# Keys of the first two token pairs from tokens times scale, the shift's part added as a row

## The reference

```
xm = rmsnorm(x, norm_w) * (1 + scale) + shift          # 4096 x 1024
k  = rope2d(xm @ w_k)                                  # 512 of w_in's columns, heads of 64
v  = xm @ w_v
state_b = sum over the tokens of the other half of gamma^m * k_m (x) v_m
```

## Time and profile before

| | |
|---|---|
| time, median of 3 runs | 877.23 us (876.34 to 927.11) |
| the profiled execution: time, span of its slowest core | 877.3 us, 875.7 us |
| spans of the eight cores | 870.9 to 875.7 us |
| PE busy | 800.4 us, 91% of the span |
| DVE, ACT, POOL busy | 465.4, 360.7, 330.8 us |
| chain that ended last | PE 80%, DMA 6%, ACT 5%, DVE 4%, issue 3% |
| of it, loads of ada_w | 4% |

### The profile page before, as it was taken

How to read it: one execution, slowest core, us unless ns; L and a number is a source line. 1 busy time by engine, 2 the same in 40 slices (tenths; PEclk the granted TensorE clock), 3 DMA queues, 4 the chain that set the end, 5 groups by cost and what they waited for, 6 DMA issues and landing times.

```text
span 875.7 us, 14323 instructions; the slowest of 8 cores (870.9 to 875.7 us)
## 1 busy us (share of the span) xinstructions
PE 800.4 (91%) x4504; PEld 384.6 (44%) x4504; DVE 465.4 (53%) x1090; ACT 360.7 (41%) x642; POOL 330.8 (38%) x372
## 2 busy tenths in 40 slices
PE   0079999999988999999999999999999999999996
PEld 0045445444444444444444444444444444444443
DVE  2457534899778777767623442344256412333435
ACT  3589646898466435343432122122212211222222
POOL 0136523676578454545410302221143143232333
PEclk9999999999999999999999999999999999999999
DMA  8999955774391221315551715325015260034233
GB/s 244 280 290 187 212 111 97 175 156 104 55 162 35 38 54 29 55 29 78 81 86 42 118 34 96 52 46 97 1 23 122 81 112 1 25 118 148 72 120 145
DMA packets 72256, 87.83 MB, mean 100 GB/s; under 512 B 51691, under 2 KB 57963, under 8 KB 70518
## 3 DMA queue, kind: packets, MB, share of 16 engines
q1 hardware_dynamic: 66854, 59.65, 25.9%
q0 software_dynamic: 5328, 27.27, 18.9%
HBM read 93.72 MB, written 8.39 MB: 117 GB/s over the span
## 4 chain that ended last, share of the span: by engine, by line
PE 80%; DMA 6%; ACT 5%; DVE 4%; issue 3%; POOL 1%; SPq 1%; DVEq 0%; ACTq 0%; POOLq 0%
PE P L1006 53%; PE P L588 13%; PE P L1303 6%; DMA wt<-ada_w 4%; ACT tm L983 2%; DMA cm<-rope 2%; PE P L707 2%; DVE vb L1021 1%; ACT st L905 1%; PE P L828 1%; PE P L648 1%; PE P L946 1%; PE P L475 1%; PE P L691 1%; PE P L947 1%
## 5 line engine op out<-in xcount | busy, mean ns | idle before, releaser
L1006 PE MATMUL P<-xmt,vb 128*128 128x512 bf16 x1280 | 283.1, 379 | 2.8 <-DVE wt L1202 1.8
L1006 PEld LDWEIGHTS P<-xmt,vb 128*128 128x128 bf16 x1280 | 124.5, 98 | 152.6 <-issue 3.7
L588 PE MATMUL P<-wt,xmt 128*128 128x512 bf16 x688 | 158.3, 382 | 4.4 <-ACT xmt L509 3.4
L1006 PE MATMUL P<-xmt,wt 128*128 128x512 bf16 x512 | 118.8, 380 | 1.1 <-ACT wt L1157 0.9
L1205 POOL TENSOR_TENSOR kz<-tm,wt 128x1024 bf16<-128x1024 f32 x16 | 45.7, 2857 | 162.4 <-DVE wt L1202 162.4
L588 PEld LDWEIGHTS P<-wt,xmt 128*128 128x128 bf16 x688 | 65.2, 98 | 79.8 <-issue 7.5
L1006 PEld LDWEIGHTS P<-xmt,wt 128*128 128x128 bf16 x512 | 49.3, 98 | 58.3 <-issue 2.7
L1282 DVE SCALAR_TENSOR_TENSOR tm<-tm,P 128x512 f32<-128x512 f32 x32 | 22.0, 687 | 87.6 <-PE P L1006 87.6
L1158 DVE TENSOR_TENSOR wt<-P,wt 128x512 f32<-128x512 f32 x32 | 22.1, 692 | 83.4 <-ACT wt L1157 62.8
L1284 POOL TENSOR_TENSOR st<-st,tm 128x512 bf16<-128x512 bf16 x32 | 39.8, 1243 | 65.8 <-DVE tm L1282 65.8
L1006 PE MATMUL P<-vb,wt 128*128 128x512 bf16 x256 | 61.4, 386 | 0.0
(11 more groups left out here) (176 smaller groups left out, 1110.8 us busy)
## 6 DMA issues: line engine op xcount, KB each, us to landing
kz<-x SPq DMA_DIRECT2D x24, 512.0 KB, 9.2
wt<-x SPq DMA_DIRECT2D x24, 512.0 KB, 4.6
vb<-w_conv POOLq DMA_DIRECT2D x16, 512.0 KB, 8.3
out<-wt SPq DMA_DIRECT2D x15, 512.0 KB, 2.7
st<-ada_w SPq DMA_DIRECT2D x2, 2048.0 KB, 14.1
wt<-ada_w SPq DMA_DIRECT2D x2, 2048.0 KB, 28.8
vb<-w_mix POOLq DMA_DIRECT2D x8, 512.0 KB, 11.1
cm<-rope SPq DMA_DIRECT2D x33, 64.0 KB, 3.9
```

Source lines behind the costliest of these rows:

```text
L588: ins = e.matmul(pf(bank)[:, 0:wid], lhsT=lhs_x(ch, k), rhs=w[:, k, c0_:c0_ + wid], start=(k == 0), stop=(k == 7))
L1006: ins = e.matmul(pf(bank), lhsT=lhs(k), rhs=rhs(k), start=(k == 0), stop=(k == 7))
```

## The change

Blocks 2 and 3 of `ada_w` (the scale) are loaded first, blocks 0 and 1 (the shift) last, and the buffers are assigned anew so that block 2 lies where the `xc` buffers 4 to 7 come. The key weights are loaded as float32 by SP in two halves (`wk_load`) and cast by DVE and ACT (`wk_cast`), in place of the casting DMA of POOL. `dpn` is loaded later; `mask_tables` is cut in two, `mask_exponents` and the rest.

For pairs 0 and 1 `f_aff_noshift` multiplies by the scale only. `k_open` projects a chunk in two groups of four matmuls and leaves the accumulation open in banks 2 to 5. When the shift is known, it is split into two bfloat16 columns (`shi`), `f_kb` multiplies them with the key weights in 8 matmuls to two rows of 512 in bank 6, the rows are split again into `kbh` and `kbl`, and `k_close` adds them to each open bank by two matmuls with a matrix of ones. Then the four chunks are rotated by `o_krope`. The loop over p begins at 2; `g_acc` of pair 0 and of pair 1 both stand in its first round. `xmTh`, the convolution's neighbour columns, is computed by its own small operations. Pairs 2 to 7 are computed as before.

```diff
--- before.py
+++ after.py
@@ -283,7 +283,14 @@
         xc = [buf(f"xc{i}", (SZ if i < 4 else WZB - 16384) + i * 4096, [128, 1024], F32) for i in range(8)]
         xso = [buf(f"xso{i}", VB + i * 2048, [128, 1024], BF16) for i in range(16)]
         kfo = [buf(f"kfo{i}", KT + i * 1024, [128, 512], BF16) for i in range(16)]
-        adaf = [buf(f"adaf{i}", o, [128, 4096], F32) for i, o in enumerate((ST, ST + 16384, WB, WZB))]
+        adaf = [buf(f"adaf{i}", o, [128, 4096], F32) for i, o in enumerate((ST + 16384, WB, WZB, ST))]
+        wkf = [buf(f"wkf{i}", XMT + 16384 + i * 8192, [128, 2048], F32) for i in range(2)]
+
+        shi = at(TMP + 14336, [128, 8, 2], BF16)
+        own("shi", TMP + 14336, 32)
+        kbh = buf("kbh", TMP + 12288, [128, 512], BF16)
+        kbl = buf("kbl", TMP + 13312, [128, 512], BF16)
+        xh2 = buf("xh2", TMP + 14400, [128, 8, 2], F32)
         adas = [buf(f"ada{i}", KT + (i % 2) * 8192, [128, 8, 512], BF16) for i in range(4)] + \
                [buf(f"ada{4 + i}", WB + i * 8192, [128, 8, 512], BF16) for i in range(2)]
         gT = at(ST, [128, 8, 576], BF16)
@@ -356,10 +363,15 @@
             P.op("dve", lambda e: e.tensor_copy(out=v[:, 0:2048], in_=adaf[i][:, 0:2048]), reads=[f"adaf{i}"], writes=[nm[0]])
             P.op("act", lambda e: e.activation(out=v[:, 2048:4096], in_=adaf[i][:, 2048:4096], func=AF.Copy), reads=[f"adaf{i}"], writes=[nm[1]])
 
-        P.dma("sp", lambda e: e.dma_start(out=dpn, in_=dpn_d[:, :]), "dpn", writes=["dpn"])
-        for i in range(3):
-            ada_load(i)
-        P.dma("pool", lambda e: e.dma_start(out=wk, in_=wk_d.rearrange("p (k c) -> p k c", k=8)), "wk", reads=["adaf2"], writes=["wk"])
+        def wk_load(q):
+            P.dma("sp", lambda e: e.dma_start(out=wkf[q], in_=wk_d[:, q * 2048:(q + 1) * 2048]), f"wkf{q}", writes=[f"wkf{q}"])
+
+        def wk_cast(q):
+            v = wk[:, 4 * q:4 * q + 4, :].rearrange("p k c -> p (k c)")
+            own(f"wk{q}d", WGB + q * 4096, 2048)
+            own(f"wk{q}a", WGB + q * 4096 + 2048, 2048)
+            P.op("dve", lambda e: e.tensor_copy(out=v[:, 0:1024], in_=wkf[q][:, 0:1024]), reads=[f"wkf{q}"], writes=[f"wk{q}d"])
+            P.op("act", lambda e: e.activation(out=v[:, 1024:2048], in_=wkf[q][:, 1024:2048], func=AF.Copy), reads=[f"wkf{q}"], writes=[f"wk{q}a"])
 
         P.op("dve", lambda e: e.tensor_copy(out=identb, in_=identf), reads=["identf"], writes=["identb"])
 
@@ -401,7 +413,7 @@
 
         P.op("act", lambda e: e.activation(out=scT, in_=vT[:, :, 0:2], func=AF.Silu), reads=["vT"], writes=["scT"])
 
-        def mask_tables():
+        def mask_exponents():
             def f_marg0(e):
                 ins = None
                 for h in range(8):
@@ -427,8 +439,10 @@
                     ins = e.scalar_tensor_tensor(out=marg[:, h, :], in0=iv, scalar=col, in1=marg[:, h, :], op0=ALU.mult, op1=ALU.subtract)
                 return ins
             P.op("dve", f_marg3, reads=["nlg", "dpn", "marg"], writes=["marg"])
+            P.op("dve", lambda e: e.tensor_scalar(out=diag, in0=identf, scalar1=1.0, scalar2=None, op0=ALU.add), reads=["identf"], writes=["diag"])
+
+        def mask_tables():
             P.op("act", lambda e: e.activation(out=marg, in_=marg, func=AF.Exp), reads=["marg"], writes=["marg"])
-            P.op("dve", lambda e: e.tensor_scalar(out=diag, in0=identf, scalar1=1.0, scalar2=None, op0=ALU.add), reads=["identf"], writes=["diag"])
 
             def f_mt(e):
                 ins = None
@@ -482,6 +496,27 @@
                 blk, j = ch["xm"]
                 P.dma("sp", lambda e, ch=ch, blk=blk, j=j: e.dma_start_transpose(out=xm[blk][:, :, j * 128:(j + 1) * 128], in_=ch["xs"][0]),
                       f"tx{ch['n'] % 4}", reads=[ch["xs"][1]] + list(after), writes=[f"xm{blk}_{j}"])
+
+        def f_aff_noshift(pair):
+            blk, j0 = pair[0]["xm"]
+            dst = xm[blk]
+            names = [f"xm{blk}_{j0}", f"xm{blk}_{j0 + 1}"]
+
+            def f_d(e):
+                ins = None
+                for k in range(4):
+                    ins = e.tensor_scalar(out=dst[:, k, j0 * 128:(j0 + 2) * 128], in0=pb(0)[:, k * 256:(k + 1) * 256],
+                                          scalar1=Amod[:, k, 0:1], scalar2=None, op0=ALU.mult)
+                return ins
+
+            def f_a(e):
+                ins = None
+                for k in range(4, 8):
+                    ins = e.activation(out=dst[:, k, j0 * 128:(j0 + 2) * 128], in_=pb(1)[:, (k - 4) * 256:(k - 3) * 256],
+                                       func=AF.Copy, scale=Amod[:, k, 0:1])
+                return ins
+            P.op("dve", f_d, reads=["Amod", "P0"], writes=[n_ + "d" for n_ in names])
+            P.op("act", f_a, reads=["Amod", "P1"], writes=[n_ + "a" for n_ in names])
 
         def f_aff(pair, inplace=False):
             r = 1 if pair[0]["kind"] == "ctx" else 0
@@ -611,33 +646,94 @@
                 return ins
             P.op("dve", f_modT, reads=[f"P{bank}", "vT"], writes=[name])
 
+
+        ada_load(2)
         load2(0)
+        ada_load(3)
+        wk_load(0)
+        wk_load(1)
+        P.dma("sp", lambda e: e.dma_start(out=dpn, in_=dpn_d[:, :]), "dpn", writes=["dpn"])
+        load2(1)
+        ada_load(0)
         rope2(0)
-        ada_load(3)
-        load2(1)
         rope2(1)
+        ada_load(1)
+        ada_cast(2)
+        ada_mm(2, 7, 0)
+        load2(2)
+        rope2(2)
+        load2(3)
+        sq2(0)
+        scale2(0)
+        load2(4)
+        f_tp(other[0])
+        for half in range(2):
+            P.op("dve", lambda e, half=half: e.tensor_copy(out=xh2[:, half * 4:half * 4 + 4, :],
+                                                           in_=pb(half).rearrange("p (a b) -> p a b", a=4)[:, :, 0:2]),
+                 reads=[f"P{half}"], writes=["xh2"])
+        ada_cast(3)
+        ada_mm(3, 7, 0)
+        modT_part((1,), "modT1", 7, 0)
+        P.op("dve", lambda e: e.tensor_scalar(out=Amod, in0=modT[:, 8:16, :], scalar1=1.0, scalar2=None, op0=ALU.add),
+             reads=["modT1"], writes=["Amod"])
+        P.op("dve", lambda e: e.tensor_tensor(out=Amod, in0=Amod, in1=vT[:, :, 2:3].broadcast_to([128, 8, 2]), op=ALU.mult),
+             reads=["Amod", "vT"], writes=["Amod"])
+        wk_cast(0)
+        f_aff_noshift(other[0])
+        wk_cast(1)
+
+        def k_open(ch, bank, part):
+            def f(e):
+                ins = None
+                for k in range(4 * part, 4 * part + 4):
+                    ins = e.matmul(pf(bank), lhsT=lhs_x(ch, k), rhs=wk[:, k, :], start=(k == 0), stop=False)
+                return ins
+            P.op("pe", f, reads=[xname(ch) + "da"[part], f"wk{part}d", f"wk{part}a"], writes=[f"P{bank}"])
+
+        def k_close(bank):
+            def f(e):
+                e.matmul(pf(bank), lhsT=onesb[0:2, :], rhs=kbh[0:2, :], start=False, stop=False)
+                return e.matmul(pf(bank), lhsT=onesb[0:2, :], rhs=kbl[0:2, :], start=False, stop=True)
+            P.op("pe", f, reads=["onesb", "kbh", "kbl"], writes=[f"P{bank}"])
+
+        for part in range(2):
+            for c in range(2):
+                k_open(other[0][c], 2 + c, part)
+        mask_exponents()
+        sq2(1)
+        scale2(1)
+        load2(5)
+        f_tp(other[1])
         ada_cast(0)
         ada_mm(0, 7, 0)
+        f_aff_noshift(other[1])
+        for part in range(2):
+            for c in range(2):
+                k_open(other[1][c], 4 + c, part)
+        mask_tables()
         ada_cast(1)
         ada_mm(1, 7, 0)
-        mask_tables()
-        ada_cast(2)
-        ada_mm(2, 7, 0)
-        sq2(0)
-        scale2(0)
-        ada_cast(3)
-        ada_mm(3, 7, 0)
-        load2(2)
-        load2(3)
-        modT_part((0, 1), "modT", 7, 0)
-        P.op("dve", lambda e: e.tensor_scalar(out=Amod, in0=modT[:, 8:16, :], scalar1=1.0, scalar2=None, op0=ALU.add),
-             reads=["modT"], writes=["Amod"])
-        P.op("dve", lambda e: e.tensor_tensor(out=Amod, in0=Amod, in1=vT[:, :, 2:3].broadcast_to([128, 8, 2]), op=ALU.mult),
-             reads=["Amod", "vT"], writes=["Amod"])
-        f_tp(other[0])
-        f_aff(other[0])
-        sq2(1)
-        scale2(1)
+        modT_part((0,), "modT", 7, 0)
+
+        def f_shi(e):
+            return e.tensor_copy(out=shi[:, :, 0], in_=modT[:, 0:8, 0])
+
+        def f_slo(e):
+            return e.tensor_tensor(out=shi[:, :, 1], in0=modT[:, 0:8, 0], in1=shi[:, :, 0], op=ALU.subtract)
+        P.op("dve", f_shi, reads=["modT"], writes=["shi"])
+        P.op("dve", f_slo, reads=["modT", "shi"], writes=["shi"])
+
+        def f_kb(e):
+            ins = None
+            for k in range(8):
+                ins = e.matmul(pf(6)[0:2, :], lhsT=shi[:, k, :], rhs=wk[:, k, :], start=(k == 0), stop=(k == 7))
+            return ins
+        P.op("pe", f_kb, reads=["shi", "wk"], writes=["P6"])
+        P.op("dve", lambda e: e.tensor_copy(out=kbh[0:2, :], in_=pf(6)[0:2, :]), reads=["P6"], writes=["kbh"])
```

(29 more changed lines are left out.)

## The result

| | before | after |
|---|---|---|
| time, median of the runs on one chip | 877.16 us | 892.57 us |
| ratio, 95% interval | | 1.0177 [1.0162, 1.0191] |
| profiled execution: time, span of its slowest core | 877.3, 875.7 us | 892.8, 891.3 us |
| PE busy | 800.4 us | 813.7 us |

What follows compares the result with a forecast made beforehand. PE was taken to bound the kernel from about 60 us on, so the head's delay counts whole: pair 3's first K projection moves from 70.05 to 79.7, and 877.3 + 9.7 = 887.0 us, range 880 to 893.

Steps and rivals of the forecast that it cites:

- POOL's pair behind two `kfo`: Pair 2's two small POOL operations queue behind kfo0 and kfo1, delaying its scale; K of pair 2 starts at 68.75.
- the marker: Start of the first K projection of pair 3: 70.05 us before, forecast 79.7, so +9.7 us.
- rival 3: Slower by more than 2%: starved PE stays below 2.4 GHz in the pass, +36 us, 923; chance 0.04.
- T = 47.6: Landing of the last ada_w block, now block 1, in us; the middle between 46.6 and 48.6.
- counting rope rows by bytes, 0.26 MB at the queue's rate: In the load queue ahead of the last ada_w block, the rope rows were counted as 0.26 MB at 0.32 MB/us.
- The step that the casting load cost no more than a plain one: In the load queue: 0.32 MB/us with the cast load beside, 0.314 and 0.34 without, so no gain from SP.
- PE has just run K of pair 1, so warm: The shift row's 8 matmuls behind T run at full pace, 1.89 us; the other end adds 1.7.
- as the second POOL wait covers it: Ahead of the marker, half pace costs little: pair 3 at 79.7, warm 79.2, since POOL's second wait hides it.
- Behind the marker all is as before, per pair: From pair 3 to the end a pair costs 6.07 us and the shift of 9.7 reaches the end whole.
- for the `kfo` alone: DVE and GpSimd blocking could delay each kfo beside a rope up to 0.4, sum 1.5 higher; nothing was added.
- The pass's ragged end: Idle time at 103.47 and a low clock from 105 to 110 could win back 3.5 us at most.
- The two 2-partition operations: Behind the shift's row, two DVE operations on 2 partitions of 512 from PSUM: 0.6 + 0.7 us with gaps.

Runs made afterwards that it cites:

- the third experiment: The changed kernel with the four rope rows of pairs 0 and 1 loaded behind the last ada_w block: 889.70 us, ratio 1.0153.
- e1: The changed kernel with sq2(2) and scale2(2) written ahead of the ropes of chunks 0 and 1: 888.96 us, ratio 1.0152.
- e2: The changed kernel without the shift's row, its split and the closings (keys of pairs 0 and 1 lack the shift): 888.02 us, ratio 1.0136.
- e7: The changed kernel with useless matmuls (12, 3, 6 and 28) put into PE's idle time: 893.19 us, ratio 1.0190.
- the fourth experiment: The kernel before with only w_k loaded as float32 on SP behind the fourth ada_w block, cast by DVE and ACT: 875.92 us, ratio 1.0003.
- the ninth experiment: The changed kernel with one added dependency, POOL's multiply in chunk 5's retention waiting for DVE's eighth operation: ratio 1.0157.
- the fourth to sixth: On the fourth experiment, the fifth makes POOL's multiply wait for DVE's eighth operation: 874.25 us, 0.9972; the sixth also casts w_k wholly on DVE: 872.64 us, 0.9961.
- the eighth: The fourth experiment plus the POOL wait, w_k cast wholly on DVE, and pair 0's rope rows loaded behind pair 1's x chunks: 874.52 us, ratio 0.9971.
- the tenth: The changed kernel with rope rows later, pair 2 projected ahead of the ropes, POOL's pairs ahead of the kfo's, and the port order pinned: 877.36 us, ratio 1.0005.

## Why the prediction was right, and where it was not

The time came inside the range and on the side forecast, and the mechanism was the one named: POOL's pair behind two `kfo`, PE's 7.39 us ahead of the transposes (forecast 7), ACT's 12.01. Pair by pair behind the marker a pair costs 6.08 (86.19 to 92.27), as forecast, so rival 3 did not come. But 887.0 was 5.6 short, and 892.57 stands only 0.4 under the upper end of 893; that it stands there is partly luck, since the loss behind the marker was no term of the range. By the medians over the cores 6.9 us are missing (16.5 instead of the forecast 9.7), in three terms:

1. **The landing, T = 47.6, came at 49.3.** The step that failed is counting rope rows by bytes, 0.26 MB at the queue's rate. The four small loads took 2.1 us by the median of after's cores instead of 0.8; that is 1.3 of the 1.7, and the third experiment puts their worth at some 2 us. What the rest is stays open: the same order of loads landed the block at 48.3 to 49.7 in after, e1, e2 and e7. The rate of the rest was right: block 1 follows the last rope row by 6.8 us in after, 2.1 MB at 0.31 MB/us. The step that the casting load cost no more than a plain one held: by the Trainium skill, "DMA: Bandwidth & Descriptors", section "Issuing engine by pattern", DMAs of sync are generally faster; this case does not show it, since in the fourth experiment the last row of the set lands at 47.7 with `w_k` as a plain load, and at 47.7 in before.

2. **From T to the marker: forecast 32.1, measured 35.1.** I wrote "PE has just run K of pair 1, so warm" and gave the row 1.89; it took 3.37. K of pair 1 itself had taken 5.69 for 16. The row ran at 2.9 to 3.6 on seven of the eight cores. And I let the transposes of the second round and K of chunk 1 run at full pace, "as the second POOL wait covers it": 1.86 and 3.16 instead of 1.06 and 1.89, ahead of the marker and covered by nothing. Read core by core, this is the split: the first K of pair 2 starts 22.4 us behind the landing by the median (forecast 21.2), and 21.3 on core 4, the only one whose row ran in 1.89. From there to the marker, forecast 11.0, cores 0 to 2 take 10.6 to 11.0, with the second transposes in 1.05 and K of chunk 1 in 1.89; the other five, at half pace, take 12.5 to 13.1. The seventh experiment warmed the row and the first transposes and won only 0.9 at the marker, since PE fell back in the wait for ACT.

3. **Behind the marker: forecast 0, measured 2.2.** "Behind the marker all is as before, per pair" was wrong in two places. One is the port at 306 us, 1.8 to 3 us by the ninth experiment. The prediction had weighed the rule of the Trainium skill ("SBUF — State Buffer", section "Who interferes with whom") for the `kfo` alone, and more loosely than the page has it: a DVE instruction with two inputs in SBUF contends with a GpSimd instruction that reads SBUF, one with a single input there, outside the 2-port perf modes, does not, and the one that starts first holds the shared pair for its whole instruction. For the `kfo` it was right to add nothing: L755 took 1032 to 1056 ns. The three rope operations beside it read PSUM and only one operand from SBUF, and the fourth, L617, which reads two, ran beside no `kfo` on any core. L1131 reads two operands from SBUF, and there this case's trace agrees with the rule: 2387 ns instead of 746. I did not look there, since nothing was changed there. The other place is the first retention product, core 3 of after, PE:

```profile
255.21 0.22 PE L1056 MATMUL P<-vb,ex 128*128 128x128 bf16 x1 [2.12 <-DVE ex L1043]
...
256.44 4.95 PE L1116 MATMUL P<-xmt,wt 128*128 128x512 bf16 x16
```

In before the gap is 1.76 and the 16 matmuls behind it take 3.62. The gap of 2.12 stands in the changed kernel and in the first, second, third, seventh and ninth experiment, that of 1.76 in the fourth to sixth, the eighth and the tenth. DVE's rope there starts 0.60 us behind the end of the K matmuls that it reads, 0.25 in before; what holds it was not found. Matmul for matmul against core 3 of before, core 3 of after loses 1.7 us at 256 to 259, where its pace is down, loses 3.1 at 306 to 314, half of it gap and half pace, and wins 1.5 back at 367, against before's own collision. The median over the cores comes to only 2.2, since cores 0, 4 and 5 of before lose 1.7 us near 435 us and no core of after does.

The pass's ragged end gave 0.4 back, of the 3.5 allowed. The two 2-partition operations took 0.68 each, as estimated.

The chance of 0.05 for slower by over 2% was low for what came: the interval ends at 1.0191. That two per cent is about what a measurement can tell here was wrong too: the interval is 0.15% to either side. The three misses had one sign, and in each I had taken a duration or a pace over from before for work that now met another neighbour.

## What to carry to other kernels

Bringing work forward is worth nothing unless the work that it leaves last is cheaper than what stood there: here 7 us between the last landing and the first matmul became a chain of a row, four closings and four ropes, with the next pair's two small operations queued behind it. When steps are written into a new order, write down each engine's queue, that of the small helper operations above all. And when a whole program shifts by some microseconds, look for pairs of operations on DVE and POOL that start within a tenth of a microsecond of each other: their order can turn over, as it did here in two chunks, one for the worse and one for the better, and one read that pins it is a cheap edit. The kernel that one starts from can hold such a pair as well.

## What the runs showed of the hardware

- A DVE operation on two operands in SBUF took 2387 ns instead of 746 when a POOL multiply of 64x1024 float32 had started 0.07 us ahead of it; with the order the other way POOL's took 2.28 us instead of 1.90. Every core of before shows it at 344 to 347 us, every core of after at 302 to 308.
- Four loads of 64 KB in a full queue took 1.0 to 2.9 us in after, 2.1 by the median of the cores, beside 6.8 us for a block of 2 MB (core 7). In before four such loads, two and two, took 0.9 to 1.9, 1.4 by the median.
- PE's clock fell after an idle time of 2.12 us on seven cores of after (4.95 us for 16 matmuls on core 3 instead of 3.62), and did not on core 0, which took 3.62; after 1.76 in the same place of before it fell on no core. After an idle time of 3.28 us in the fourth experiment cores 1, 3 and 6 ran the next 8 matmuls in 1.89. The length of the gap alone does not decide.
- The clock column of before shows 1.00 from 44 to 60 us, while its first eight K matmuls took 3.53 us there; those of after at 73.14 took 3.57, and there the column shows 0.50. The length of the matmuls says more than the column.
